# Every sixth slab of weights as 120 rows and 8 rows, in a two-block transformer kernel with a gathered expert layer

## What is computed

```python
def peer(xn, wq, k1, k2, u_tab, v_tab):
    ...
    v1, i1 = lax.top_k(s1, TOPK)
    v2, i2 = lax.top_k(s2, TOPK)
    cand = (v1[..., :, None] + v2[..., None, :]).reshape(t, PEER_HEADS, TOPK * TOPK)
    sv, ci = lax.top_k(cand, TOPK)
    ...
    def chunk(args):
        xi, ei, gi = args
        hid = jax.nn.gelu(jnp.einsum("td,tkd->tk", xi, u_tab[ei]))
        return jnp.einsum("tk,tkd->td", gi * hid, v_tab[ei])
```

## Time and profile before

| | |
|---|---|
| median of 3 runs | 2013.53 us (2012.8 to 2015.92) |
| the profiled execution, its own time | 2013.99 us |
| its span, first to last instruction | 2012.2 us |
| busy: PE, DVE, ACT, POOL | 1755.2, 1288.1, 870.8, 581.0 us |
| moved by DMA | 772.23 MB, mean 384 GB/s over the span |
| gathers, slabs and other loads | 536.90 MB, 233.95 MB on their queues |
| mean granted TensorE clock | 0.981 of full speed |

### The profile page before, as it was taken

The page is one execution under the profiler, slowest core; times in us unless marked ns, Lnnn a source line. Parts: engine busy times, 40 slices in busy tenths (PEclk is TensorE's granted clock), DMA queues, the critical chain, the costliest instruction groups (busy, mean ns, idle before and its releaser), DMA issues.

```text
span 2012.2 us, 21668 instructions
## 1 busy us (share of the span) xinstructions
PE 1755.2 (87%) x7096; PEld 995.0 (49%) x7096; DVE 1288.1 (64%) x3503; ACT 870.8 (43%) x2184; POOL 581.0 (29%) x517
## 2 busy tenths in 40 slices
PE   9999999999999988887779987977899898777776
PEld 4449865763577465464226534622464364222222
DVE  4224337677865367686876857688586677874444
ACT  2423214344488344723353473344437534443333
POOL 0000000023322233333443334344433334443331
PEclk9999999999999999999999988999999999999999
DMA  9769877499999999999999999999999999999996
GB/s 382 260 266 362 300 278 252 157 339 402 419 419 419 420 420 420 419 419 412 420 419 408 420 405 417 420 419 419 420 419 420 386 419 420 420 420 420 420 420 258
DMA packets 109105, 772.23 MB, mean 384 GB/s; under 512 B 12224, under 2 KB 12736, under 8 KB 17088
## 3 DMA queue, kind: packets, MB, share of 16 engines
q0 software_dynamic: 73728, 536.90, 64.7%
q1 hardware_dynamic: 35264, 233.95, 30.1%
HBM read 769.75 MB, written 1.05 MB: 383 GB/s over the span
## 4 chain that ended last, share of the span: by engine, by line
DMA 46%; PE 40%; DVE 6%; issue 4%; ACT 4%; SPq 0%; POOL 0%; DVEq 0%; POOLq 0%; ACTq 0%
DMA ring<-in_peer_dram,eidx 15%; DMA arena<-in_peer_dram,eidx 12%; PE psum L1189 11%; PE psum L772 10%; DMA kv<-in_peer_dram,eidx 9%; PE psum L795 8%; DMA ring<-in_slabs_dram 6%; DMA early<-in_peer_dram,eidx 5%; PE psum L1001 4%; PE psum L1018 2%; DVE ring L2118 1%; DVE arena L2118 1%; ACT diag L1534 1%; PE psum L972 1%; PE psum L870 1%
## 5 line engine op out<-in xcount | busy, mean ns | idle before, releaser
L2269 POOL DMA_INDIRECT arena<-in_peer_dram,eidx x206 | 229.0, 1112 | 839.1 <-DVE eidx L1990 427.8
L1189 PE MATMUL psum<-arena,diag 128*128 128x512 f32 x740 | 363.9, 618 | 80.9 <-ACT diag L1534 77.3
L1524 ACT ACTIVATE wexp<-wexp 128x1 f32<-128x1 f32 x512 | 103.2, 202 | 674.7 <-DVE wexp L2118 669.6
L2118 DVE CUSTOM_DVE_ANT_0 arena<-arena,osb 128x1024 f32<-128x1024 f32 x206 | 251.7, 1222 | 142.7 <-DMA arena<-in_peer_dram,eidx 140.6
L1189 PE MATMUL psum<-ring,diag 128*128 128x512 f32 x520 | 255.0, 615 | 42.0 <-ACT diag L1534 40.1
L1189 PEld LDWEIGHTS psum<-arena,diag 128*128 128x128 f32 x740 | 132.7, 193 | 272.8 <-ACT diag L1534 150.3
L2118 DVE CUSTOM_DVE_ANT_0 ring<-ring,osb 128x1024 f32<-128x1024 f32 x152 | 185.7, 1223 | 124.4 <-DMA ring<-in_peer_dram,eidx 122.0
L772 PE MATMUL psum<-ring,hT 128*128 128x512 f32 x528 | 241.5, 604 | 13.5 <-DMA ring<-in_slabs_dram 11.3
L2269 POOL DMA_INDIRECT ring<-in_peer_dram,eidx x152 | 175.3, 1153 | 252.7 <-PE psum L1189 189.7
L1189 PE MATMUL psum<-kv,diag 128*128 128x512 f32 x364 | 178.6, 613 | 42.8 <-ACT diag L1534 37.0
L1534 ACT ACTIVATE diag<-const,wexp 128x128 f32<-128x128 f32 x450 | 180.7, 402 | 16.6 <-PE psum L1189 1.9
(11 more groups left out here) (338 smaller groups left out, 2019.6 us busy)
## 6 DMA issues: line engine op xcount, KB each, us to landing
ring<-in_slabs_dram SPq DMA_DIRECT2D x199, 1024.0 KB, 5.7
ring<-in_slabs_dram SPq DMA_DIRECT2D x8, 768.0 KB, 4.2
kept<-in_slabs_dram SPq DMA_DIRECT2D x4, 1024.0 KB, 13.3
arena<-in_peer_dram,eidx POOLq DMA_INDIRECT x206
ring<-in_slabs_dram SPq DMA_DIRECT2D x6, 512.0 KB, 6.8
ring<-in_peer_dram,eidx POOLq DMA_INDIRECT x152
kk<-in_keys_dram SPq DMA_DIRECT2D x2, 1024.0 KB, 9.1
kv<-in_peer_dram,eidx POOLq DMA_INDIRECT x102
```

What stands on the lines that cost most here:

```text
L1189: ins = pe.matmul(bank(b), diags_of(n), pair(slot_of[n])[:, 1024 + 512 * h:1536 + 512 * h], start=(k == 0), stop=(k == 127))
L1524: act.activation(wn, wn, ACT.Gelu_apprx_tanh).then_inc(*up("gelu", n))
L2118: v.tensor_tensor_reduce(out=row, in0=row, in1=row_y[t], scale=1.0, scalar=0.0, op0=ALU.mult, op1=ALU.add, accum_out=wexp[:, c:c + 1]).the ...
L2269: pool.indirect_dma_start(pair(i), None, tables, bass.IndirectOffsetOnAxis(ap=eidx[:, 128 * t + k:128 * t + k + 1], axis=0)).then_inc(sig. ...
```

## The change

A function `parted(n)` is true for each sixth slab number from the first gather on. Such a slab is loaded by two transfers instead of one, issued by SP right after each other: the first 120 partitions, then the last 8. `filled` counts two for it, so that PE's wait covers both.

```diff
+        def parted(n):
+            return n >= less[0] and n % 6 == 0
+
         def filled(n):
-            return sum(place(m) == place(n) for m in range(n + 1))
+            return sum(1 + parted(m) for m in range(n + 1) if place(m) == place(n))
...
-                sp.dma_start(slot(n)[:, 0:width], T["slabs"][i][:, 0:width]).then_inc(sig.sem("slab%d" % place(n)), 16)
+                for rows in (slice(0, 120), slice(120, 128)) if parted(n) else (slice(0, 128),):
+                    sp.dma_start(slot(n)[rows, 0:width], T["slabs"][i][rows, 0:width]).then_inc(sig.sem("slab%d" % place(n)), 16)
```

## The result

| | before | changed |
|---|---|---|
| median, 4 runs each | 2013.6 us | 2096.68 us |
| lowest to highest | 2012.8 to 2015.92 | 2095.79 to 2098.77 |
| span of a profiled execution | 2012.2 us | 2097.0 us |

The ratio is 1.0414, with a 95% interval of 1.0402 to 1.0427. The changed kernel is 83 us slower, 4.6 us for each of the 18 split slabs, where 7 us less was forecast.

The account below looks back on a forecast made before the run. The prediction took the DMA engines, one about 8 us behind, to bound the kernel. Its terms, -8.4 - 5.9 + 5.4 + 1.8 = -7.1 us, gave a median of 2006.4 us, range 2000.5 to 2021.5.

Parts of the forecast that it names:

- What bounds the kernel: From about 500 us the 16 DMA engines never rest, at some 419 GB/s; one ends about 8 us behind.
- How the rows are spread: In each split slab, 120 rows fill 15 engines and 8 rows go one each to eight engines.
- The spared engine is the late one: In split slabs, the engine left out by 120 rows was taken to be the one about 8 us behind.
- It has 43 us of relief: Over the split slabs, the engine 8 us behind would be spared 43 us of work and be level by the end.
- the ninth row: Extra row per split slab for each of eight engines, a loss of 5.4 us charged in full.
- the tail's gain: After 1990 us, the last data shared by all 16 engines would land 8.4 us sooner.
- the dips: Four short rate falls between 500 and 1640 us, after gaps in POOL's gathers; filling them was to gain 5.9 us.
- the third rival: The wrong engine is spared: 2018.9 us if the slow one is among the eight, otherwise 2013.5; chance 0.07.
- The odd shapes: Transfers of 120 or 8 rows in split slabs: loss of 0.1 us each, 1.8 us in all; upper bound 39 us.
- The rival of crowded writes: Engines of split slabs slow one another writing neighbouring partitions: 0.94 us more a piece, 2021.5 us; chance 0.18.
- Costs nothing: 18 more issues on SP, 5.9 us over 1200 us, and PE's semaphore count of 32 would add no time.

Follow-up runs that it names:

- near: Kernel before plus 24 loads of 8 rows into the neighbouring partitions 0 to 7, which nothing reads: 2042.15 us.
- far: Kernel before plus 24 loads of 8 rows into partitions 0, 4, ... 28, which nothing reads: 2019.45 us.
- the column run: Changed kernel with each split slab cut into two transfers of 128 rows and half the width instead of 120 and 8 rows: 2015.29 us.
- the halves: Changed kernel with the 18 split slabs cut as 64 and 64 rows instead of 120 and 8: 2082.45 us.

## Why the prediction was wrong

**What bounds the kernel: right.** Twelve added loads of 1 MB cost 30.2 us where 30 were expected. 7.5 us of work on four engines, the late one among them, cost 7.3, while the same on two others was free. DMA sets the end, and of its engines the late one does.

**How the rows are spread: right.** 15 and 8 engines, by the small packets.

**The spared engine is the late one: wrong.** The prediction called this the step that no row shows, and built both gains on it (-8.4 and -5.9) with a chance of 0.07 for the opposite. "It has 43 us of relief" was asserted, and the tails of the changed kernel and of the run with only 120 rows show one engine as late as before. The late engine got the ninth row instead. So the tail's gain is zero, and the dips have not shrunk: 283 and 216 GB/s in windows of 5 us, with no split slab near. Alone this would have given the third rival's time, 2018.9 us (2020.7 with the 1.8 us for the shapes, which the prediction left out there).

**The odd shapes: the term that missed by some 76 us.** I put 0.1 us a slab, 1.8 in all, with 2.2 a slab as the upper bound. With the gains at zero and the ninth row's 5.4 as charged, 83.1 - 5.4 = 77.7 us are left for it, 4.3 a slab. With the 14.3 us of gains that did not come, that makes the 90 us between forecast and measurement. There were two faults. The bound was made from the 8-row piece alone and held the 120-row transfer to be free, while that one costs 3.7 of the 4.6 us that a split slab costs in all. And the value was taken near the lower end because slabs and gathers mix at a full 419 GB/s; but all those rows were of 128-row transfers, and say nothing of another shape. The rival of crowded writes had the right mechanism and, for the piece itself, nearly the right size: 0.94 us expected, 0.95 measured between near and far. It gave the large transfer, which it mentions in half a sentence, no price.

**The sum as measured.** 120-row transfers 66.3 us, less 2.7 us for bytes left out in that run, make 63.6. The 8-row pieces add 19.1. 63.6 + 19.1 = 82.7, beside 83.1. How the 19.1 divide is not shown: 5.4 for the ninth row would leave 13.7, or 0.8 each, for crowding, beside 0.95 for the added near pieces. In the tail of the changed kernel the other seven engines with a ninth row are not behind (254 GB/s, then 53), as the eight are in the run with far pieces:

```profile
1996.00:1998.00 2.00, 1.50 (x4) 0.49 (x3) 0.75 (x3) 0.90 (x3) 0.00 (x0) 1.00 0.56 233
1998.00:2000.00 2.00, 1.62 (x4) 0.38 (x2) 1.07 (x2) 0.83 (x3) 0.00 (x0) 1.00 0.47 197
```

So part of the 5.4 may have been covered where the split slabs slowed everything.

**Costs nothing: right** for the issues and the semaphore (the column run). **Said of the profile of after:** the sign for crowding was a DMA share of 1.01 with the rate under 410 near split slabs, and the sign for the wrong engine the row at 25 to 29 GB/s; both are there.

Open: what sparing the late engine would bring was not tried. No transfer shape found here takes rows from just that engine without sending others across. So it is also not shown whether the dips depend on its lag. Why that engine is late isn't shown either. Nor is the exact pattern of a 120-row transfer. That its engines share groups of partitions as the 8-row pieces do is inferred from the pieces, from the loss that stays with 16 engines, and from the halves. But for the large transfers the rows read and the partitions written were not tested apart, and the halves lost more than the estimate from ports. None of the runs is faster than the kernel before.

## What to carry to other kernels

Where DMA is full, load whole slabs of 128 partitions, and cut along columns if a load has to be cut (here into rows of 4 KB); a cut along rows slowed the gathers in flight too, not just its own transfer. When the DMA share is 1.0 but the GB/s are low, look first for transfers of fewer than 128 partitions, whose engines may write into one another's. Before a change that rebalances engines, find out which one is late by weighing down a few at a time, and see whether the end moves.

## What was not expected of the hardware

- Loads of 120 rows in place of 128 took the total rate from 420 to 256 GB/s while they were in flight; 112 + 16 rows cost 3.2 us a slab, 64 + 64 rows 3.8 us, 120 + 8 rows 4.6 us, columns nothing.
- 24 pieces of 8 rows ended 5 to 7, 15 and 27 to 28 us late with one, two and four engines for each group of four partitions written, as if engines in one group shared one engine's rate. Which rows of HBM they read moved the time by 2 us at most.
- The late engine takes part in four-row transfers but not in two-row ones. The Trainium skill ("DMA: Bandwidth & Descriptors", section "Latency and other measured facts") names engines 7 and 15 as usually slower. If the rows go to the lowest-numbered engines, the late one here is neither, since a four-row load (+7.3 us) reaches it.
